# A fifth open quad of experts, and column pieces of 512, 512, 512, 256 and 256 in the last stage of a float32 MoE layer

## What is computed

```
g_w, g_idx = top_k(softmax(t @ w_rg + b_rg), 1)          # 4 groups
e_top, e_idx = top_k(logits of the group's 8 experts, 2) # 32 experts in all
for e in range(32):
    hdn = silu(t @ w1[e]) * (t @ w3[e])                  # [256, 512]
    out += combine[:, e:e+1] * (hdn @ w2[e])             # w2[e] is [512, 2048]
h = h + out
gate = sigmoid(rmsnorm(h, g_pg) @ w_pg + b_pg)           # w_pg is [2048, 2048]
h = h + gate * rmsnorm(p @ w_ple, g_ple)
```

## Time and profile before

| | |
|---|---|
| three timed runs | 1388.9, 1390.49, 1395.16 us; median 1390.49 |
| profiled execution, its own time | 1387.55 us |
| its span | 1385.8 us |
| granted TensorE clock, mean | 0.902 |
| PE busy | 1090.6 us, 79% of the span |
| DVE busy | 285.4 us, 21% |
| ACT busy | 156.7 us, 11% |
| DMA | 476.16 MB, mean 344 GB/s |

### The profile page before, as it was taken

How to read it: one execution, slowest core, us unless ns; L and a number is a source line. 1 busy time by engine, 2 the same in 40 slices (tenths; PEclk the granted TensorE clock), 3 DMA queues, 4 the chain that set the end, 5 groups by cost and what they waited for, 6 DMA issues and landing times.

```text
span 1385.8 us, 13825 instructions
## 1 busy us (share of the span) xinstructions
PE 1090.6 (79%) x6016; PEld 505.3 (36%) x6016; DVE 285.4 (21%) x439; ACT 156.7 (11%) x314; POOL 53.5 (4%) x66
## 2 busy tenths in 40 slices
PE   8999999999875787666765666666576666889998
PEld 4458887445522233222221223222232212333333
DVE  1103726412321212121221121000000000110116
ACT  1111315002200012000000000000000000010102
POOL 0112110200000002000000000000000000000000
PEclk9999999999897899888888889888887878999999
DMA  9943334354599999999999999999999999999971
GB/s 353 303 152 122 122 122 151 130 213 182 210 426 427 429 426 428 427 427 428 428 427 428 428 425 428 414 429 427 414 427 418 426 426 411 387 394 386 396 285 61
DMA packets 91054, 476.16 MB, mean 344 GB/s; under 512 B 10272, under 2 KB 10416, under 8 KB 67952
## 3 DMA queue, kind: packets, MB, share of 16 engines
q1 hardware_dynamic: 84896, 471.88, 84.1%
q0 software_dynamic: 560, 2.88, 0.6%
q10 hardware_dynamic: 5536, 0.47, 0.3%
HBM read 473.12 MB, written 2.10 MB: 343 GB/s over the span
## 4 chain that ended last, share of the span: by engine, by line
DMA 50%; PE 48%; SPq 1%; issue 1%; DVE 1%; ACT 0%; DVEq 0%
DMA ring<-in_w 48%; PE ps L1421 8%; PE ps L1850 6%; PE ps L1384 6%; PE ps L1676 6%; PE ps L1545 4%; PE ps L1753 4%; PE ps L1558 4%; PE ps L1808 2%; DMA area<-in_w 2%; PE ps L1646 2%; PE ps L1821 1%; PE ps L1639 1%; SPq L386 1%; PE ps L1578 1%
## 5 line engine op out<-in xcount | busy, mean ns | idle before, releaser
L1753 PE MATMUL ps<-ring,area 128*32 128x512 f32 x1024 | 167.0, 800 | 121.5 <-DMA ring<-in_w 121.0
L1676 PE MATMUL ps<-ring,area 128*32 128x512 f32 x976 | 150.1, 736 | 127.8 <-DMA ring<-in_w 127.8
L1184 DVE TENSOR_TENSOR h<-ps,h 128x2048 f32<-128x2048 f32 x32 | 73.3, 2292 | 301.9 <-PE ps L1646 301.9
L1753 PEld LDWEIGHTS ps<-ring,area 128*32 128x32 f32 x1024 | 43.5, 139 | 232.1 <-issue 232.1
L1676 PEld LDWEIGHTS ps<-ring,area 128*32 128x32 f32 x976 | 31.9, 124 | 225.8 <-issue 225.6
L1421 PE MATMUL ps<-hT,ring 128*128 128x256 f32 x512 | 112.9, 380 | 0.0
L1421 PEld LDWEIGHTS ps<-hT,ring 128*128 128x128 f32 x512 | 96.6, 190 | 14.0 <-issue 1.2
L1850 PE MATMUL ps<-ring,area 128*128 128x512 f32 x192 | 90.2, 612 | 5.4 <-DMA ring<-in_w_pg 3.9
L1384 PE MATMUL ps<-ring,hT 128*128 128x512 f32 x192 | 84.8, 601 | 1.1 <-DVE hT L907 1.1
L1229 DVE TENSOR_TENSOR hT<-area,ps 128x128 f32<-128x128 f32 x16 | 4.6, 288 | 316.0 <-ACT area L860 316.0
L1639 PE MATMUL ps<-area,hs 128*128 128x128 f32 x512 | 65.7, 284 | 0.5 <-DVE area L1165 0.5
(11 more groups left out here) (278 smaller groups left out, 784.9 us busy)
## 6 DMA issues: line engine op xcount, KB each, us to landing
ring<-in_w SPq DMA_DIRECT2D x157, 2048.0 KB, 21.5
ring<-in_w SPq DMA_DIRECT2D x57, 1024.0 KB, 16.1
ring<-in_w_in SPq DMA_DIRECT2D x28, 1024.0 KB, 12.7
ring<-in_w_out SPq DMA_DIRECT2D x16, 1024.0 KB, 7.2
ring<-in_w_pg SPq DMA_DIRECT2D x12, 1024.0 KB, 15.7
area<-in_w SPq DMA_DIRECT2D x2, 2048.0 KB, 14.0
hs<-in_w SPq DMA_DIRECT2D x4, 1024.0 KB, 14.2
hs<-in_w_pg SPq DMA_DIRECT2D x3, 1024.0 KB, 16.2
```

What stands on the lines that cost most here:

```text
L1184: dve.tensor_tensor(h[:, t, :], ps[:, bank:bank + 4, :].rearrange("p b n -> p (b n)"), h[:, t, :], ALU.add).then_inc(acc_done, 1)
L1676: ins = mm(ps[SLOTS * g:SLOTS * g + SLOTS, 0, :], XG[:, b, k, SLOTS * e:SLOTS * e + SLOTS], s[:, D_EXP * kk:D_EXP * kk + D_EXP], start=(k ...
L1753: ins = mm(ps[SLOTS * g:SLOTS * g + SLOTS, 0, :], XG[:, b, k, SLOTS * e:SLOTS * e + SLOTS], s[:, D_EXP * kk:D_EXP * kk + D_EXP], start=(k ...
```

## The change

`OPEN_QUADS` goes from 4 to 5, so the quad of experts 12 to 15 is read and computed in the open form. `WIDTHS` replaces four pieces of 512 columns by 512, 512, 512, 256 and 256. A chunk of a narrow piece still fills one place, with two k tiles of 256 columns; it is read by two transfers of 512 KB, with 512 rows of 1 KB each. A narrow piece gives 2 k tiles of the gate (`K_TILES`) instead of 4, so its gate units have 2 matmuls. `HDNs` is longer, so the scatter matrix of quad 4 moves to `area`, and the one `Y` buffer replaces the two `Ys`: ACT's copy of a quad's output now waits until the scatter of the quad before has read it. The gate units are dealt to five quads as 2, 1, 2, 1, 1, and the eighth after the last scatter. `FIRST_XG` only sets with which of two buffers the open quads begin.

```diff
-OPEN_QUADS = 4
+OPEN_QUADS = 5
...
-PIECES = 4
+WIDTHS = (512, 512, 512, 256, 256)
+PIECES = len(WIDTHS)
+PIECE_AT = tuple(sum(WIDTHS[:i]) for i in range(PIECES))
+K_TILES = tuple(w // P for w in WIDTHS)
+PER_PLACE = tuple(512 // w for w in WIDTHS)
+W2_CHUNKS = tuple(4 // n for n in PER_PLACE)
+FIRST_XG = FULL_QUADS % 2
...
+def gate_units(q):
+
+    return range(-(-7 * q // OPEN_QUADS), -(-7 * (q + 1) // OPEN_QUADS))
...
-                sp_q.dma_start(places[place].rearrange("p (e n) -> p e n", e=QUAD),
-                               w2_v[e:e + QUAD, :, k, 512 * i:512 * i + 512].rearrange("e p n -> p e n")
-                               ).then_inc(open_loaded[place], 16)
+                width, at = WIDTHS[i], PIECE_AT[i]
+                for r in range(PER_PLACE[i]):
+                    sp_q.dma_start(places[place][:, QUAD * width * r:QUAD * width * (r + 1)].rearrange("p (e n) -> p e n", e=QUAD),
+                                   w2_v[e:e + QUAD, :, PER_PLACE[i] * k + r, at:at + width].rearrange("e p n -> p e n")
+                                   ).then_inc(open_loaded[place], 16)
...
-                act.wait_ge(open_used, w2_used(i, q, 3))
-                if m >= 2:
-                    act.wait_ge(piece_ps, m - 1)
-                act.activation(Ys[:, m % 2, :], ps[:, 4 + m % 2, :], ACT.Copy).then_inc(y_copied, 1)
+                act.wait_ge(open_used, w2_used(i, q, W2_CHUNKS[i] - 1))
+                if m >= 1:
+                    act.wait_ge(piece_ps, m)
+                act.activation(Y[:, 0:WIDTHS[i]], ps[:, 4 + m % 2, 0:WIDTHS[i]], ACT.Copy).then_inc(y_copied, 1)
...
                     for e in range(QUAD):
-                        ins = mm(ps[SLOTS * e:SLOTS * e + SLOTS, 4 + m % 2, :], HDNs[:, QUAD * q + e, k, :],
-                                 rows[:, 512 * e:512 * e + 512], start=(k == 0), stop=(k == 3))
-                    ins.then_inc(open_used, 1)
+                        ins = mm(ps[SLOTS * e:SLOTS * e + SLOTS, 4 + m % 2, 0:width], HDNs[:, QUAD * q + e, k, :],
+                                 rows[:, width * e:width * e + width], start=(k == 0), stop=(k == 3))
+                    if k % PER_PLACE[i] == PER_PLACE[i] - 1:
+                        ins.then_inc(open_used, 1)
...
-                for kk in range(4):
+                for kk in range(K_TILES[i]):
                     rows = in_place("w_pg", i, kk, 0)
                     ins = mm(ps[:, u % 2, :], hT_pieces[:, i % 2, kk, P * t:P * t + P], rows[:, 512 * n:512 * n + 512],
-                             start=(kk == 0), stop=(kk == 3))
+                             start=(kk == 0), stop=(kk == K_TILES[i] - 1))
```

More of the change, by code:

```diff
@@ L98, in open_pair_used, with piece_begins @@
     return QUAD_CHUNKS * q + in_quad
+def piece_begins(i):
+    return OPEN_CHUNKS + sum(OPEN_QUADS * W2_CHUNKS[a] + K_TILES[a - 1] for a in range(1, i))
 def w2_used(i, q, k):
@@ L116, in piece_loads @@
     for i in range(1, PIECES):
[L117 to L120, removed]
+        w2_ = [("w2", i, q, k) for q in range(OPEN_QUADS) for k in range(W2_CHUNKS[i])]
+        w_pg_ = [("w_pg", i - 1, kk, 0) for kk in range(K_TILES[i - 1])]
+        order += w_pg_ + w2_ if i == 1 else w2_[:W2_CHUNKS[i]] + w_pg_ + w2_[W2_CHUNKS[i]:]
+    return order + [("w_pg", PIECES - 1, kk, 0) for kk in range(K_TILES[-1])]
 def place_pieces():
@@ L140, in place_pieces @@
         after, uses = free[place]
-        placed[load] = (place, after, uses + 1)
-        free[place] = (w2_used(i, q, k) if what == "w2" else w_pg_used(i, q), uses + 1)
+        uses += PER_PLACE[i] if what == "w2" else 1
+        placed[load] = (place, after, uses)
+        if load[:2] != ("w_pg", PIECES - 1):
+            free[place] = (w2_used(i, q, k) if what == "w2" else w_pg_used(i, q), uses)
+        else:
+            del free[place]
     return placed
@@ L171, in build @@
         br_bc = sb("br_bc", [P, NL])
-        pieces = sb("pieces", [P, 2, NT, 4])
+        pieces = sb("pieces", [P, 2, NT, PIECES])
         r_ple = sb("r_ple", [P, NT])
@@ L260, in build @@
         HDNs = hT_flat[:, 0:OPEN * 4 * SLOTS].rearrange("p (j k s) -> p j k s", j=OPEN, k=4)
-        Gs = hT_flat[:, 2048:2048 + OPEN_QUADS * T].rearrange("p (q t m) -> p q t m", q=OPEN_QUADS, t=NT)
-        Ys = hT_flat[:, 3072:4096].rearrange("p (b n) -> p b n", b=2)
+        G_HOMES = [hT_flat[:, 2560 + T * q:2560 + T * q + T] for q in range(4)] + [part(10240, T)]
+        Gs = [g_.rearrange("p (t m) -> p t m", t=NT) for g_ in G_HOMES]
+        Y = hT_flat[:, 3584:4096]
         ahead_places = [area[:, 10496:10496 + 2 * CH], area[:, 4096:4096 + 2 * CH], hT_flat[:, 0:2 * CH]]
@@ L459, in w_pg_load @@
                 sp_q.wait_ge(open_used, after)
-                sp_q.dma_start(places[place], w_pg_v[:, 4 * i + kk, :]).then_inc(open_loaded[place], 16)
+                sp_q.dma_start(places[place], w_pg_v[:, PIECE_AT[i] // P + kk, :]).then_inc(open_loaded[place], 16)
             for what, i, q, k in piece_loads():
@@ L1273, in _ @@
                     dve.wait_ge(pe_raw, 8)
[L1274 removed]
+                    step(dve.tensor_reduce(ss[:, 4:6], pieces[:, 1, :, 0:4], AX, ALU.add))
                     dve.tensor_scalar(ss[:, 4:6], ss[:, 4:6], 1.0 / D, EPS, ALU.mult, ALU.add).then_inc(msp_ready, 1)
@@ L1300, in add_piece @@
                 for t in range(NT):
-                    piece = h[:, t, 512 * i:512 * i + 512]
-                    dve.tensor_tensor(piece, ps[:, 6 + t, :], piece, ALU.add).then_inc(h_final, 1)
+                    piece = h[:, t, PIECE_AT[i]:PIECE_AT[i] + WIDTHS[i]]
+                    dve.tensor_tensor(piece, ps[:, 6 + t, 0:WIDTHS[i]], piece, ALU.add).then_inc(h_final, 1)
             def copy_turned(i):
                 dve.wait_ge(turn_ps, 2 * i + 2)
-                for kk in range(2, 4):
-                    dve.tensor_scalar(hT_pieces[:, i % 2, kk, :], ps[:, 3, T * (kk - 2):T * (kk - 2) + T],
-                                      gain(1, 4 * i + kk), None, ALU.mult).then_inc(turn_dve, 1)
+                half = K_TILES[i] // 2
+                for kk in range(half, 2 * half):
+                    dve.tensor_scalar(hT_pieces[:, i % 2, kk, :], ps[:, 3, T * (kk - half):T * (kk - half) + T],
+                                      gain(1, PIECE_AT[i] // P + kk), None, ALU.mult).then_inc(turn_dve, 2 // half)
             def gate_landed(i, u):
                 if u == 7 and i < PIECES - 1:
-                    dve.wait_ge(open_used, w_pg_used(i, 3))
+                    dve.wait_ge(open_used, w_pg_used(i, K_TILES[i] - 1))
                 else:
@@ L1830, in turn_piece @@
                 for half in range(2):
-                    for u in range(2):
+                    for u in range(K_TILES[i] // 2):
                         for t in range(NT):
-                            k = 4 * i + 2 * half + u
+                            k = PIECE_AT[i] // P + K_TILES[i] // 2 * half + u
                             ins = pe_.transpose(ps[:, 2 + half, T * u + P * t:T * u + P * t + P], h[:, t, P * k:P * k + P], ident[:, :])
@@ L1895, in _ @@
                             scatter_piece(i, q - 1)
-                    gate_unit(i - 1, 2 * q)
-                    if q < OPEN_QUADS - 1:
-                        gate_unit(i - 1, 2 * q + 1)
+                    for u in gate_units(q):
+                        gate_unit(i - 1, u)
                     if i == 1:
```

40 lines of the change are left out of this document (21 added, 19 removed).

## The result

The changed kernel takes 1395.62 us (median of 20 runs, 1393.31 to 1398.69) against 1388.31 us of the kernel before (20 runs beside it, 1387.55 to 1395.62). The ratio is 1.0041, with a 95% interval of 1.0033 to 1.005: 5.7 us of 1388. Measured a second time it was 1.0034 (1.0021 to 1.0046), 4.7 us. The forecast was +4.9 us, 1395.4.

A forecast was written before the change was run, and what follows sets the result against it. Reads bound the kernel until PE's last w2 wait, then PE's work and the finish: landing 1275.0 plus 80.8 plus 34.85 ends at 1390.65, +4.9 us on 1385.8; on the timed median 1395.4, range 1389 to 1404.

The forecast's parts named there:

- the second term: PE's work from the last wide w2 load's landing to the last scatter's end: 80.8 us, against 32.8 before.
- The landing of the last wide load: First term: the last chunk of piece 2, quad 4, PE's last wait, lands 38.5 us earlier, at 1275.0.
- rival "faster": In the wide pieces, places come free too late; five quads free them sooner: -6.5 us, 1384, chance 0.06.
- rival "narrow blocks do not halve": Narrow w2 blocks on PE take more than 1.90 us: 6.7 us more, at the bound 16.7; chance 0.08.
- The finish: Third term, from the last scatter's end to the span's end: 34.85 us against 39.45, units 2.84 apart by DVE's chain.
- The clock: Rival: PE's clock falls to half level in the last units, up to 4.7 us more, 1400; chance 0.07.
- 1 KB rows: Narrow w2 reads at 3.03 us a MiB; rival: dearer than that, 6.6 us more at 3.4, chance 0.20.
- The tie: At the last scatter's end, the reads as bound give 1355.1 and PE's work 1355.8.
- Transfers of 512 KB: Forty in place of 20 of 1 MiB for the narrow pieces: expected to cost nothing, fixed part hidden by surrounding transfers.

The follow-up runs named there:

- experiments 3 and 4: DVE's base step for the next unit put ahead of its sigmoid wait: 3 in the changed kernel, ratio 1.001; 4 in the kernel before, 1.0003.
- experiment 6: Changed kernel with the narrow w2 loads in rows of 512 bytes, four transfers of 256 KB per place: ratio 1.0117 to the kernel before.
- Experiment 7: Changed kernel without 14 of the 32 gate matmuls of piece 2, 12 us less PE work: ratio 1.0024 to the kernel before.
- experiment 5: Changed kernel with 2 KB rows in the narrow pieces' reads, same bytes and 512 KB transfers: ratio 1.0031 to the kernel before.
- the pair: Changed kernel with both the 2 KB rows of experiment 5 and the 14 fewer gate matmuls of Experiment 7: ratio 0.9984 to the kernel before.

## Why the prediction was right

The sum came out for its stated reasons. Behind the copy of ACT the change costs 5.8 us in the profile, by the ratios 4.7 to 5.7; the forecast was 4.9. Most of the 0.9 between is in the second term.

- **The landing of the last wide load.** 38.5 us earlier was forecast, 38.50 was measured (913.80 - 875.30). The rates that it used, 427 and 386 to 390 GB/s, held, and so did the choice of the load. SP's waits are still there, with the same sum as in the earlier trace rows:

```profile
SPq L475 <- PE ps L1834: 53.0, 23, 5.2
```

  So the rival "faster" (free places come too late) had no part: with a fifth quad the waits stayed at 53 us, at no cost in rate.
- **PE's work behind it.** 80.8 forecast, 81.45 measured, twice (81.6 by the chain's mark). A narrow block took 1.86 and not 1.90, but a gate stretch ahead of a w2 block takes 0.1 more than I counted, eight times, and twice of these 0.2, where it also stands behind a w2 block (7.07 for 6.87 from 1292.18 to 1299.25). The rival "narrow blocks do not halve" is out.
- **The finish.** 34.85 forecast, 35.1 measured (34.9 by the chain's mark). Units are 2.84 apart; experiments 3 and 4 show that this is DVE's chain, and that it counts only where PE's unit is shorter.
- **The clock** did fall, to 0.50 from 1369.8 to 1375.5, and cost nothing: the two banks were full when it fell, and DVE's 2.84 a unit went on. The rival named the fall rightly and its own counterargument as well. It did not see that a shorter chain on DVE would make the fall count: 1.47 us in experiment 3.
- **1 KB rows** were put at 3.03 us a MiB and took 3.00. The Trainium skill (DMA: Bandwidth & Descriptors, Why small descriptors are slow) had given 2.84 by its 3 cycles a packet, and by the same rule rows of 512 B would take 2.72 x 76/67 = 3.09 (both are estimates from the page); experiment 6 measured 3.62. The measurement decides: the fixed part of a row is larger here.
- **The tie** was right in kind; the margin was put at 0.7 us (1355.1 against 1355.8). Experiment 7 has it at 2.15, experiment 6 at 1.7.
- **Transfers of 512 KB.** SP issued them without becoming the limit:

```profile
L475 SPq DMA_DIRECT2D ring<-in_w x63: 433/2246/11694, 1139.6 to 1343.9; - x63
...
DMA to landing us min/median/max: 6.8/14.2/23.7
```

  The shortest issue took 0.43 us; the median of 2.25 is SP held back, as in the earlier trace rows. The Trainium skill (DMA: Bandwidth & Descriptors, Rules for kernel authors) wants 1 MiB or more; 386 GB/s with 512 KB (experiment 5) against 386 with 1 MiB says that it makes no difference while others are in flight.

What the prediction left out is that its two parts don't add: the fifth quad is worth 0 by itself and some 3 to 4 us beside the narrow pieces (1.0062 against 1.0034 to 1.0041, and 4.0 by the sections). It had taken the change as one sum and so could not have said which half to keep.

## What to carry to other kernels

A smaller last piece shortens the tail only down to the pace of whoever finishes the tail: before moving work ahead of the last step, look at the distance of the finishing units, not at PE's share of them. Here 13.7 us of PE's work were moved out of a place that hid all but 2 us of their saving into one where each counted. Where two resources are near a tie, test one edit of each kind and both together: single edits gave 0 and 2 us, the pair 7. To compare two profiles within a few microseconds, start from an event that both share shortly before the change, since the parts ahead of it can differ by 4 us (the copy stands at 399.72 to 404.06 in these profiles, and 2 us apart in the two of the changed kernel).

## What had not been expected of the hardware

The price of a read follows one line over a range of 32 in row length. A MiB took 2.46 us in 64 rows of 16 KB, 2.72 in 512, 3.00 in 1024 and 3.62 in 2048 rows of 512 B, some 0.0006 us a row throughout, with the DMA share rising from 1.01 to 1.05, 1.10 and 1.20. Two transfers for a MiB in place of one left no trace in it (386 GB/s with the same rows, experiment 5); four were tried only together with rows of 512 B, and that point lies on the line too.
